# Key and value projection of the opening done feature by feature among the queries

## The reference, cut to what matters

```
m_lat = split(silu(c) @ ada_w[0] + ada_b[0], 6)          # m_ctx likewise from c_ctx
h     = modulate(x, m[0], m[1])                          # x * (1 + scale) + shift, 512 tokens
qa, ka, va, qb, kb, vb = split(h @ ev_w_in)              # 512, 128, 128, 512, 512, 512 columns
qa = rope(rms_norm(qa, q_gain)); ka = rope(rms_norm(ka, k_gain))     # rope on latent tokens only
```

## Time and profile before

| what | us |
|---|---|
| median of three executions | 1576.27 |
| span of the profiled execution, first to last instruction | 1572.0 |
| TensorE busy in that span | 1543.6 (98%) |
| VectorE, ScalarE, GpSimd busy | 1067.6, 880.8, 337.9 |

### The profile page before, as it was taken

One profiled execution on the slowest core, in us unless ns is written; L12 is line 12 of the kernel. 1 busy time (PEld: TensorE's weight loads), 2 busy tenths in 40 slices (PEclk: granted clock), 3 DMA queues, 4 the chain that ended last, 5 costly groups with the idle time before them and its releaser, 6 DMA issues.

```text
span 1572.0 us, 25520 instructions
## 1 busy us (share of the span) xinstructions
PE 1543.6 (98%) x9936; PEld 1319.7 (84%) x9936; DVE 1067.6 (68%) x1983; ACT 880.8 (56%) x1735; POOL 337.9 (21%) x340
## 2 busy tenths in 40 slices
PE   7999999999999999999999999999999999999998
PEld 4788778988887888887999988988888898888886
DVE  4743766666444525788787768777888668779874
ACT  2423873666652423568455555756766557567662
POOL 0201420355540000112011102242221014412210
PEclk9999999999999999999999999999999999999999
DMA  9766123345657224021545562424555534335551
GB/s 369 301 238 243 21 82 134 122 182 205 236 226 261 81 108 152 13 79 68 186 177 218 184 231 105 144 104 164 187 189 187 202 142 154 139 137 188 187 202 78
DMA packets 46951, 260.35 MB, mean 166 GB/s; under 512 B 11888, under 2 KB 13168, under 8 KB 18160
## 3 DMA queue, kind: packets, MB, share of 16 engines
q1 hardware_dynamic: 43952, 252.78, 43.7%
q0 software_dynamic: 1296, 4.72, 0.8%
q10 hardware_dynamic: 1584, 1.23, 0.2%
HBM read 257.64 MB, written 1.07 MB: 165 GB/s over the span
## 4 chain that ended last, share of the span: by engine, by line
PE 90%; DVE 4%; ACT 3%; DMA 2%; issue 1%; POOL 0%; SPq 0%; DVEq 0%; ACTq 0%
PE ps L512 22%; PE ps L513 21%; PE ps L514 21%; PE ps L764 8%; PE ps L765 5%; PE ps L667 2%; PE ps L689 2%; PE ps L676 2%; PE ps L528 2%; PE ps L1164 1%; PE ps L766 1%; DMA raw<-in_ada 1%; PE ps L575 1%; DMA raw<-in_ev_w_in 1%; PE ps L1191 1%
## 5 line engine op out<-in xcount | busy, mean ns | idle before, releaser
L1931 DVE TENSOR_TENSOR wl<-raw,wh 128x1024 fp32r<-128x1024 f32 (+2 forms) x304 | 357.5, 1217 | 249.9 <-ACT wh L1437 248.6
L1437 ACT CAST wh<-raw 128x1024 fp32r<-128x1024 f32 (+1 forms) x318 | 313.6, 1036 | 337.0 <-PE ps L514 302.3
L512 PE MATMUL ps<-xx,wh 128*128 128x256 f32 (+1 forms) x1006 | 328.1, 326 | 0.0
L514 PE MATMUL ps<-xx,wl 128*128 128x256 f32 (+1 forms) x1006 | 325.5, 324 | 0.0
L513 PE MATMUL ps<-xx,wh 128*128 128x256 f32 (+1 forms) x1006 | 325.5, 324 | 0.0
L512 PE MATMUL ps<-wh,xx 128*128 128x512 f32 (+2 forms) x780 | 285.9, 367 | 2.7 <-DVE xx L2356 1.2
L514 PE MATMUL ps<-wh,xx 128*128 128x512 f32 (+2 forms) x780 | 281.1, 360 | 0.0
L513 PE MATMUL ps<-wl,xx 128*128 128x512 f32 (+2 forms) x780 | 281.0, 360 | 0.0
L2302 DVE SCALAR_TENSOR_TENSOR arena<-ps,pv,arena 128x254 f32<-128x254 f32 (+2 forms) x352 | 192.9, 548 | 28.7 <-ACT arena L1637 19.3
L512 PEld LDWEIGHTS ps<-xx,wh 128*128 128x128 f32 x1006 | 189.9, 189 | 20.1 <-issue 4.0
L514 PEld LDWEIGHTS ps<-xx,wl 128*128 128x128 f32 x1006 | 189.9, 189 | 15.2
(11 more groups left out here) (242 smaller groups left out, 2234.9 us busy)
## 6 DMA issues: line engine op xcount, KB each, us to landing
raw<-in_ada SPq DMA_DIRECT2D x46, 1024.0 KB, 5.0
raw<-in_up SPq DMA_DIRECT2D x44, 1024.0 KB, 4.9
raw<-in_fin SPq DMA_DIRECT2D x44, 1024.0 KB, 4.8
raw<-in_down SPq DMA_DIRECT2D x22, 1024.0 KB, 4.8
raw<-in_fout SPq DMA_DIRECT2D x22, 1024.0 KB, 4.8
raw<-in_win SPq DMA_DIRECT2D x12, 1024.0 KB, 4.9
raw<-in_ev_w_in SPq DMA_DIRECT2D x9, 1024.0 KB, 7.4
raw<-in_wout SPq DMA_DIRECT2D x8, 1024.0 KB, 4.9
```

Of the source, the lines that this page charges most:

```text
L512: e.matmul(out, A[0], B[0], start=first, stop=False)
L514: return e.matmul(out, A[1], B[0], start=False, stop=last)
L1437: e.copy(hi_of(j)[:, a:b], raw_of(j)[:, a:b]).then_inc(*S.hi.up((j, half)))
L1931: e.tensor_tensor(lo_of(j)[:, a:b], raw_of(j)[:, a:b], hi_of(j)[:, a:b].bitcast(F), ALU.subtract).then_inc(*S.lo.up((j, half)))
```

## The change

Chunk 2 (kv) is loaded behind chunk 1, ahead of `ada` chunks 3 and 7, and split behind feature 5 on both engines into a place of its own in `home`. TensorE multiplies it feature by feature in the opening (`early_kv`), 12 matmuls of 256 columns for each feature, into banks 5 and 0; the block `tokens` of chunk 2 is gone. `ada(3, ...)` and its finish now stand behind `first(5)`, among the kv products. Parts of `first(1)` and `first(2)` are moved between the `ada` products and their finish. Features are cast and subtracted in halves of 256 tokens and TensorE waits for the half of its tile; VectorE makes feature and low part of one before the next. Split 3 on ScalarE moves from behind feature 5 to behind feature 7. `LATER` becomes (2, 2, 3, 3, 2, 2, 2). The order of tiles and splits becomes

```diff
-LATER = (2, 2, 2, 2, 2, 2, 2, 2)
+LATER = (2, 2, 3, 3, 2, 2, 2)
-    o = ada(0, 0, 4) + ev(0) + ada(0, 1, 5, 2, 6) + ev(1) + ada(0, 3, 7)
+    o = ada(0, 0, 4) + ev(0) + ada(0, 1, 5, 2, 6) + ev(1, 2) + ada(0, 3, 7)
-    for i, few in zip((3, 4, 2, 5, 6, 7), LATER):
+    for i, few in zip((3, 4, 5, 6, 7), LATER):
-    SPLITS = [j for j, o in enumerate(ORDER) if o[3] == "split"]
+    KV = J["ev_w_in", 2]
+    SPLITS = [j for j, o in enumerate(ORDER) if o[3] == "split" and j != KV]
+    HOME = {KV: (10240, 12288), ...
+    KV_BANK = (5, 0)
+        def early_kv(k, tiles=t4):
+            hv, lv = (v.rearrange("p (k n) -> p k n", k=8)[:, k, :] for v in (hi_of(KV), lo_of(KV)))
+            q.wait_ge(*S.hi.at((KV, k // 4)))
+            q.wait_ge(*low_done(KV, k // 4))
+            for t in tiles:
+                wait_token_feature(k, t)
+                tk = slice(128 * t, 128 * t + 128)
+                out = ps[KV_BANK[t // 2]][:, 256 * (t % 2):256 * (t % 2) + 256]
+                m = mm3(out, (xh[:, k, tk], xl[:, k, tk]), (hv, lv), k == 0 and t % 2 == 0, k == 7 and t % 2 == 1)
+                ...
         ada(1, 0)
+        first(1, (0,))
         ada(1, 1)
-        first(1, (0, 1))
+        first(1, (1,))
         ada_finish(1)
         first(1, (2, 3))
         ada(2, 0)
         first(2, (0, 1))
         ada(2, 1)
-        first(2, (2, 3))
+        first(2, (2,))
         ada_finish(2)
-        first(3)
+        first(2, (3,))
+        for k in (3, 4, 5):
+            first(k)
+        early_kv(0)
         ada(3, 0)
-        first(4, (0, 1))
+        early_kv(1)
         ada(3, 1)
-        first(4, (2, 3))
+        early_kv(2, (0,))
         ada_finish(3)
-        for k in (5, 6, 7):
+        early_kv(2, (1, 2, 3))
+        for k in (3, 4, 5):
+            early_kv(k)
+        for k in (6, 7):
             first(k)
+        for k in (6, 7):
+            early_kv(k)
+        nb[0] = 0
 ...
-        bs = tokens("ev_w_in", 2, "kv", t4, turns=False)
-        ada_few()
 ... ScalarE and VectorE alike:
-        for tile in QK[0:2]:
+        for tile in QK[0:4]:
             qk(tile)
         weights(after(J["ev_w_in", 1]))
-        for tile in QK[2:4]:
+        for tile in QK[4:12]:
             qk(tile)
         copies_qb(copy, 0)
         weights(after(J["ev_w_in", 3]))
-        for tile in QK[4:8]:
-            qk(tile)
         copies_qb(copy, 1)
         weights(after(J["ev_w_in", 4]))
-        for tile in QK[8:12]:
-            qk(tile)
-        weights(after(J["ev_w_in", 2]))
         copies_kb(copy, 0)
```

More of the change, by code:

```diff
@@ L585, in wait_feature, with wait_token_feature @@
             q.wait_ge(*S.xl.at((key, k)))
+        def wait_token_feature(k, t):
+            q.wait_ge(*S.xh.at(("f0", k, t // 2)))
+            q.wait_ge(*S.xl.at(("f0", k, t // 2)))
         def tokens(name, i, key, tiles, xkey=None, turns=True, beside=lambda t, k: None):
@@ L834, in first @@
                     m.then_inc(*S.proj.up(("use", j)))
+        def early_kv(k, tiles=t4):
[3 more added lines that the diff above has]
+            for t in tiles:
+                wait_token_feature(k, t)
+                tk = slice(128 * t, 128 * t + 128)
+                out = ps[KV_BANK[t // 2]][:, 256 * (t % 2):256 * (t % 2) + 256]
+                m = mm3(out, (xh[:, k, tk], xl[:, k, tk]), (hv, lv), k == 0 and t % 2 == 0, k == 7 and t % 2 == 1)
+                if k == 7 and t % 2:
+                    m.then_inc(*S.proj.up(("kv", t - 1), ("kv", t), ("use", KV)))
         ada(0, 0)
@@ L852, in tensor_program @@
         ada(2, 1)
-        first(2, (2, 3))
+        first(2, (2,))
         ada_finish(2)
-        first(3)
+        first(2, (3,))
+        for k in (3, 4, 5):
+            first(k)
+        early_kv(0)
         ada(3, 0)
-        first(4, (0, 1))
+        early_kv(1)
         ada(3, 1)
-        first(4, (2, 3))
+        early_kv(2, (0,))
         ada_finish(3)
-        for k in (5, 6, 7):
+        early_kv(2, (1, 2, 3))
+        for k in (3, 4, 5):
+            early_kv(k)
+        for k in (6, 7):
             first(k)
+        for k in (6, 7):
+            early_kv(k)
         for t in t4:
             BANK["q0", t] = BANK["q1", t] = bs[t]
+            BANK["kv", t] = KV_BANK[t // 2]
             free[bs[t]] = [(S.ea, ("qk", 2 * t)), (S.ea, ("qk", 2 * t + 1))]
+        for t in t2:
+            free[KV_BANK[t]] = [(S.ea, ("va", 2 * t)), (S.ea, ("va", 2 * t + 1))]
+        nb[0] = 0
         more = iter([(n, i) for n in (4, 5) for i in range(8)])
@@ L876, in tensor_program @@
         columns("ev_w_in", 4, 512, "qb1")
-        ada_few()
-        bs = tokens("ev_w_in", 2, "kv", t4, turns=False)
-        for t in t4:
-            free[bs[t]] = [(S.ea, ("va", t))]
         ada_few()
@@ L1475, in qk @@
                 q.wait_ge(*S.vec.at((key[0], key[1] - 2)))
-            o = ps[BANK.get((bank, t), 0)][:, 256 if bank == "q1" else 0:]
+            o = ps[BANK.get((bank, t), 0)][:, 256 if bank == "q1" or bank == "kv" and t % 2 else 0:]
             e.copy(x, o[:, 0:64 * nh].rearrange("p (h d) -> p h d", h=nh)).then_inc(*S.ea.up(key))
@@ L1668, in scalar_program @@
         for k in range(8):
-            q.wait_ge(*S.vec.at(("feat", "f0", k)))
-            e.copy(xh[:, k, :], tmp[:, k % 2, :]).then_inc(*S.xh.up(("f0", k)))
+            for g in range(2):
+                w = slice(256 * g, 256 * g + 256)
+                q.wait_ge(*S.vec.at(("feat", "f0", k, g)))
+                e.copy(xh[:, k, w], tmp[:, k % 2, w]).then_inc(*S.xh.up(("f0", k, g), ("f0", k)))
             if k == 0:
@@ L1683, in scalar_program @@
             if k in (3, 5):
-                weights(SPLITS[k // 2])
+                weights(SPLITS[1] if k == 3 else KV)
+        weights(SPLITS[2])
         e.dma_start(pv[:, 96:NPV], T["pv"][:, 96:NPV]).then_inc(*S.pv.up("pv", by=16))
@@ L2350, in feature @@
                     e.tensor_scalar(tmp[:, k % 2, w], XT[:, k, w], sc[:, 0, k, g:g + 1], mods[:, 0, k, g:g + 1],
-                                    ALU.mult, ALU.add).then_inc(*S.vec.up(("feat", "f0", k)))
+                                    ALU.mult, ALU.add).then_inc(*S.vec.up(("feat", "f0", k, g)))
             def feature_low(k):
-                q.wait_ge(*S.xh.at(("f0", k)))
-                e.tensor_tensor(xl[:, k, :], tmp[:, k % 2, :], xh[:, k, :].bitcast(F), ALU.subtract).then_inc(
-                    *S.xl.up(("f0", k)))
+                for g in range(2):
+                    w = slice(256 * g, 256 * g + 256)
+                    q.wait_ge(*S.xh.at(("f0", k, g)))
+                    e.tensor_tensor(xl[:, k, w], tmp[:, k % 2, w], xh[:, k, w].bitcast(F), ALU.subtract).then_inc(
+                        *S.xl.up(("f0", k, g), ("f0", k)))
             if n == 0:
@@ L2367, in vector_program @@
                 continue
-            for k in (2 * n, 2 * n + 1):
-                feature(k)
+            feature(2 * n)
             if n == 2:
                 weights_half(SPLITS[1], 0)
-            for k in (2 * n, 2 * n + 1):
-                feature_low(k)
+            feature_low(2 * n)
+            feature(2 * n + 1)
+            feature_low(2 * n + 1)
             if n == 2:
                 weights_half(SPLITS[1], 1)
+                weights(KV)
         weights(SPLITS[2])
```

3 lines of the change are left out of this document (1 added, 2 removed).

## The result

The changed kernel takes 1586.61 us (median of six executions, 1583.35 to 1588.07) against 1576.59 for the kernel before (six, 1574.97 to 1581.22). The ratio is 1.0065 with a 95% interval of 1.0054 to 1.0076, so it is slower by 0.65%. Three later executions, one of them of e7, took 1693 us or more at a granted clock of 0.85 or lower, and the ratios leave them out. The forecast was 1584.7 with a range of 1579 to 1588. The profiled execution took 1587.14 us, its span 1585.7: 13.7 us more than the span before.

The account below looks back on a forecast made before the run. TensorE was taken to bound the kernel (busy 98%). Block 5 starting 5.5 us later and one `ada` chunk (0.93) make 6.5: 1576.3 + 6.5 = 1582.8; a slow start of 1.9 makes 1584.7, range 1579.0 to 1588.0.

Parts of the forecast that it names:

- Opening and kv end at 57.6: Opening with kv product on TensorE: over at about 57.6 instead of 59.6, a gain of 2.0 us (0 to 2.7).
- When the tiles begin: VectorE and ScalarE ahead of the tiles: angles begin 4.75 us later, so tile 0 is copied at 55.3, not 50.55.
- How long the tiles take: Twelve tiles at VectorE's pace: 34.4 us instead of 38.48 (32.7 to 35.5); split 5 behind them done at 94.6.
- What TensorE wants: TensorE reaches block 5 at 87.6, waits 7.2 us, starts at 94.8; with one `ada` chunk fewer done, 6.5 us lost.
- Slow start: TensorE after the wait at block 5: half clock for 3.7 us of work, costing 1.9 us (0 to 3.4).
- Rival (a): At block 5: the stall comes without half clock after it, total time 1582.8 us; chance 0.2.
- From there both traces run alike.: From the start of attention, expected near 143 instead of 134.76, to the end: no further difference between the kernels.
- What lies around the span: Time outside the profiled span: 4.3 us around the span of 1572.0 before, left as it is.
- (b): No stall at block 5, the new order only fills idle time in the opening: 1574.3 us; chance 0.09.
- (c): Tiles start later, from chunk 3's load or loads behind it, each us late costing one: 1586.7 with 2 us; chance 0.08.
- (d): Milder stall at block 5, tiles beginning 2 to 4 us sooner or TensorE keeping its rate: 1578 to 1581; chance 0.08.
- (e): In the opening, late split kv delays its product, 1 us late giving 1585.7; its chance is counted with (c).

Follow-up runs that it names:

- e7: e5's kernel with gate values transposed on TensorE and stored by one transfer in 512-byte pieces; 1571.94 us, ratio 0.9986 to the kernel before.
- e2: The changed kernel with unread matmuls ahead of block 5, keeping TensorE busy through the wait; 1579.74 us, ratio 1.0031.
- e1: The changed kernel with split 5 put back between tiles 7 and 8 on both engines; 1574.87 us, ratio 1.0001.
- e9: The changed kernel with gate values transposed on TensorE and stored in 512-byte pieces; 1581.5 us, ratio 1.0051.
- e6: The changed kernel with gate rows stored in another element order, gate values landing permuted, still 4-byte packets; 1582.18 us, ratio 1.0053.
- e11: e9's kernel once more, unedited, on the same chip as e10; 1582.42 us, ratio 1.0052.
- e10: The changed kernel once more, unedited, on the same chip as e11; 1583.17 us, ratio 1.0057.
- e4: The changed kernel with the four gate stores moved behind the eight bias tables on SyncE; 1588.07 us, ratio 1.0081.
- e8: The kernel before with only the gate values transposed on TensorE and stored in 512-byte pieces; 1573.64 us, ratio 1.0.
- e5: e1's kernel with one `ada` chunk moved ahead of block 4, into the bank wait; 1573.57 us, ratio 0.9999.
- e3: The kernel before with only split 5 moved behind tiles 8 to 11; 1581.11 us, ratio 1.0036.

## Why the prediction was right, and where its sizes were off

- **Opening and kv end at 57.6.** Measured 57.66. The third group's second chunk was taken as unmoved at 25.93; it went at 26.18, with a wait of 0.89 for its DMA. `ada` 7 was hidden as said: TensorE notes no wait for it. The terms given from the finish on come to 57.4 with the finish itself (43.1 + 0.4 + 8.4 + 5.5), not 57.6; the finish began at 43.29.
- **When the tiles begin.** Scale and shift at 43.6, measured 43.94; split 3 from 48.0, measured 48.06; angles at 50.35, measured 50.34; tile 0 at 55.3, measured 55.27.
- **How long the tiles take.** 34.4, measured 34.47. Tile 11 at 89.7 (89.74), the qb copy at 91.7 (91.70), split 5 done at 94.6 (94.65).
- **What TensorE wants.** Bank wait 1.3 at 73.7, measured 1.31 before 73.88; a wait of 7.2 before 94.8, measured 7.00 before 94.75. The sum of 6.5 is what e2 shows with the clock held up, 6.47. That the gain of the opening is swallowed whole is e1 against e2: the same opening gives 134.26 or 141.23.
- **Slow start.** The step was right. Its size was a little high for the execution profiled with the result and too low for the five others. From the first matmul of block 5 to attention e2 takes 46.34 us (141.23 - 94.89). The first execution of the changed kernel takes 47.92 (142.67 - 94.75), so 1.6; e9 takes 48.89 (143.30 - 94.41), so 2.55, and e6, e11, e10 and e4 come to 2.6 to 2.9 (48.97, 49.03, 49.14 and 49.22). The forecast had 1.9 with an upper bound of 3.4, a bound that it worked out from no row. In those five the lower clock lasted 10.2 us, in the first one 6.8. The rule in the Trainium skill (TensorE: Matmul & The Clock Gate, part 1 and the section on how oscillation bites in real kernels), that a long enough wait costs the array its higher clock until it has worked again, agrees with the long waits here: the granted clock is 0.50 of full from 91.3 to 98.1 in the changed kernel, 1.00 in e2, where the wait was filled, and 1.00 through the opening of the kernel before, whose longest wait is 1.71 us. But one long wait isn't the only way to lose the clock: it fell at 176.6 in the changed kernel when TensorE had been idle for 1.22 us, busy for 0.63 and idle again since 176.0. Rival (a), no slow start, is out.
- **"From there both traces run alike."** This failed in the profiled execution: 1443.0 us from attention to the end against 1437.25. It is the unforeseen term, 5.8 of the 13.7 between the spans. The forecast for the spans was 8.4, and 7.91 of it had been lost when attention began. Side by side, attention to the end takes 1437.1 to 1437.3 us in the four traces without the 4-byte stores (e7, e8, e9, e11). In the nine with them it takes 1437.2 to 1437.7 in four (the kernel before, e2, e5, e6), 1438.4 in e10, 1438.96 in e1 (1573.22 - 134.26), and 1442.0 to 1443.0 in three, all with a late split (e3, e4 and the first trace of the changed kernel). So no loss was seen without the stores, e4 moves the stores and a disturbance moves along, and with them it is a matter of the single execution. That the packets of 4 bytes are what does it is argued: the turned values also go out at another moment and behind another semaphore. In the median it is small: ratios of 1.0065 and 1.0057 with the stores, 1.0051 and 1.0052 without, so 2.2 and 0.8 us, and the intervals overlap.
- **What lies around the span.** The prediction took 4.3 us, the median less the profiled span. That mixed two executions. The execution profiled after has 1.44 around its span (1587.14 - 1585.7), and no recorded execution of the kernel before has more than about 1.5. The one profiled before then took about 1573.4, an estimate, some 2.9 faster than the median shown with it. The sum from the profile, 1572.0 + 8.4 + 1.4 = 1581.8, is what e9 and e11 measure (1581.5 and 1582.42), where nothing disturbs attention. That the forecast of 1584.7 came nearer to 1586.61 is in part luck: 2.9 us that belonged to no term stood in for a loss that the prediction didn't have. The median of before may have carried some of the same disturbance; this is argued from the narrow spread of e7 and e8 and not shown.
- **The other rivals.** (b), no stall, needed split 5 by 87.6; e1 has it there and is the case, at 1574.87 instead of 1574.3. (c), (d) and (e) did not occur: nothing in the chain to 94.65 was off by more than 0.4.

What stays open is why small stores hold TensorE's results up. In the first trace of the changed kernel one fetch of instructions (16 KB) took 2.1 us in the stretch of the stores against about 1.1 after it, and 3.4 in e3, where a loss followed, but also 4.6 in e2, 3.4 in e6 and 2.5 in the kernel before, where none did. So a delayed fetch may be part of it, but it doesn't tell the executions with a loss from those without.

## What to carry to other kernels

When work is moved into idle time on the engine that bounds, follow the orders of the other engines to the next thing that the bounding engine wants: here a gain of about 2 us was lost because one split of 2.35 us stood behind four more tiles and a copy, and 7 us of wait with up to 2.9 of half rate came of it. Place what the bounding engine needs by when it is due, not by its kind. And take the time around the span from the same execution as the span: a median from other executions put nearly 3 us into the forecast that belonged to none of its terms.

## What the runs showed of the hardware

- A wait of 7.0 us is followed by matmuls of 512 columns at 0.43 us apart instead of 0.23, for 3.4 us in one execution (94.75 to 98.1) and for 5.4 to 6.1 us in five others, of kernels that don't differ from it in this stretch (e9: 94.41 to 99.8, e4: 95.41 to 101.6). A wait of 3.67 us (e3) has the same effect for 3.4 us, and one of 1.3 us (e1, at 74 and at 167.5) has none. Two short waits, 1.22 and 1.98 us with 0.63 us of work between, went with 6.8 us at the lower clock (176.6 to 183.4).
- Beside four stores of 4 KB in packets of 4 bytes, some 4100 packets, VectorE got TensorE's results 2.60 and 3.35 us after their recorded end instead of 0.05 (173.59 and 177.46 in the changed kernel). That the stores cause it is likely by e4 and e9 and not proved. With them the executions of a kernel spread over 1 to 7 us (e1 1572.36 to 1579.02), without them over 0.7 to 1.7 (e7, e8, e9, e11). Four transposes and a copy, which don't show in the median of e8, turn them into one store.
- The order of the elements in DRAM alone doesn't set a store's packets: e6 made them neighbours there and had as many packets as before. In e7 they lie side by side in SBUF too, and 4120 packets are gone.
- The best of these kernels is e7, at 0.9986 (0.9977 to 0.9995) of the kernel before: the change's opening, split 5 in its old place, one `ada` chunk earlier, and the turned gate values.
